# Two orders of loading: which queue carries the first weights and the first tokens, and when layer 1's second slab is fetched

## The reference

```
mix, st = mixing_block(h, pos, w_in, b_in, w_s, b_s, g_mix, w_out, ...)   # starts with x @ w_in + b_in
h = layer_norm(ALPHA * h + mix, ln1_g, ln1_b)
h = layer_norm(ALPHA * h + hier_moe(h, ...), ln2_g, ln2_b)                # top-2 of 16 experts per token
```

## Time and profile before

| What | Value |
|---|---|
| Time, median of 3 runs | 1622.8 us (1620.92 to 1624.57) |
| The profiled execution's own time | 1614.26 us |
| Its span on the core | 1612.4 us |
| Time outside the span in that execution | 1.9 us |
| Mean granted TensorE clock | 0.928 of full speed |
| PE busy | 1427.5 us, 89% of the span |
| DMA, mean over the span | 195 GB/s |

### The profile page before, as it was taken

One profiled execution on the slowest core, in us unless ns is written; L12 is line 12 of the kernel. 1 busy time (PEld: TensorE's weight loads), 2 busy tenths in 40 slices (PEclk: granted clock), 3 DMA queues, 4 the chain that ended last, 5 costly groups with the idle time before them and its releaser, 6 DMA issues.

```text
span 1612.4 us, 20129 instructions
## 1 busy us (share of the span) xinstructions
PE 1427.5 (89%) x7676; PEld 801.9 (50%) x7676; DVE 730.6 (45%) x1525; ACT 313.9 (19%) x651; POOL 129.0 (8%) x118
## 2 busy tenths in 40 slices
PE   7999988889889969999499999888889996999990
PEld 3565555555554535554246454655656454455540
DVE  1294645665583331111437764467458535111116
ACT  1100022323320101121211010333324001221112
POOL 0000200100000040000200011010100001300002
PEclk9999999899889979999799999989988996999995
DMA  9116954457443249999702213553673305799984
GB/s 295 57 50 219 306 149 165 144 161 134 119 163 102 109 158 379 410 407 389 260 31 105 91 48 119 170 203 111 143 159 131 107 0 214 279 403 400 404 331 176
DMA packets 138352, 314.48 MB, mean 195 GB/s; under 512 B 52004, under 2 KB 83748, under 8 KB 117156
## 3 DMA queue, kind: packets, MB, share of 16 engines
q1 hardware_dynamic: 109488, 192.88, 33.8%
q0 software_dynamic: 12672, 86.51, 17.4%
q10 hardware_dynamic: 16116, 34.04, 5.8%
HBM read 266.05 MB, written 47.35 MB: 194 GB/s over the span
## 4 chain that ended last, share of the span: by engine, by line
PE 59%; DVE 18%; issue 14%; DMA 5%; ACT 2%; POOL 1%; ACTq 0%; POOLq 0%; DVEq 0%; SPq 0%
PE ps L1998 9%; PE ps L2344 7%; PE ps L2036 7%; DVE ring L1189 4%; PE ps L2410 4%; DVE z L1189 4%; PE ps L2142 3%; DMA kbuf<-in_cache_k,idx_k 2%; PE ps L2417 2%; PE ps L2447 2%; PE ps L1886 2%; PE ps L2105 2%; PE ps L2071 1%; PE ps L2275 1%; PE ps L1897 1%
## 5 line engine op out<-in xcount | busy, mean ns | idle before, releaser
L1189 DVE TENSOR_TENSOR z<-z,ps 128x512 f32<-128x512 f32 (+1 forms) x102 | 57.6, 585 | 280.8 <-ACT z L890 206.0
L890 ACT ACTIVATE ring<-ps 128x512 f32<-128x512 f32 (+2 forms) x186 | 95.8, 539 | 325.1 <-PE ps L2142 177.5
L2036 PE MATMUL ps<-ring,xT 128*128 128x512 f32 (+1 forms) x384 | 144.4, 535 | 0.8 <-ACT xT L890 0.8
L890 ACT ACTIVATE z<-ps 128x512 f32<-128x512 f32 (+3 forms) x137 | 71.4, 535 | 369.9 <-PE ps L2410 129.1
L2410 PE MATMUL ps<-ring,z 128*128 128x512 f32 x304 | 138.5, 609 | 2.2 <-ACT z L890 1.8
L1998 PE MATMUL ps<-ring,x 128*128 128x512 f32 x320 | 139.1, 593 | 0.0
L2036 PEld LDWEIGHTS ps<-ring,xT 128*128 128x128 f32 x384 | 73.3, 193 | 65.1 <-issue 60.5
L2142 PE MATMUL ps<-tab,kbuf 128*128 128x128 f32 x512 | 86.8, 296 | 13.0 <-DMA kbuf<-in_cache_k,idx_k 8.2
L1998 PEld LDWEIGHTS ps<-ring,x 128*128 128x128 f32 x320 | 60.5, 190 | 74.8 <-issue 74.1
L2410 PEld LDWEIGHTS ps<-ring,z 128*128 128x128 f32 x304 | 57.5, 194 | 69.2 <-issue 68.2
L1189 DVE TENSOR_TENSOR z<-ps,vbuf 128x512 f32<-128x512 f32 (+3 forms) x68 | 36.9, 542 | 112.3 <-PE ps L2036 71.3
(11 more groups left out here) (277 smaller groups left out, 2004.6 us busy)
## 6 DMA issues: line engine op xcount, KB each, us to landing
ring<-in_w SPq DMA_DIRECT2D x114, 1024.0 KB, 9.6
ring<-in_w_in SPq DMA_DIRECT2D x9, 2048.0 KB, 10.3
expert_rows<-zero SPq DMA_DIRECT2D x1, 13056.0 KB, 60.1
expert_rows<-z ACTq DMA_DIRECT2D x19, 512.0 KB, 7.9
z<-expert_rows ACTq DMA_DIRECT2D x17, 512.0 KB, 10.8
ring<-in_w_in SPq DMA_DIRECT2D x6, 1024.0 KB, 8.2
z<-expert_rows ACTq DMA_DIRECT2D x19, 256.0 KB, 8.9
expert_rows<-z ACTq DMA_DIRECT2D x38, 128.0 KB, 6.0
```

The costliest lines, as they stand in the source:

```text
L890: return nc.scalar.activation(out, in_, fn, **kw)
L1189: return V.tensor_tensor(out, a, b, op)
L2036: m = mm(ps[0:n, i % 4, 0:w], xTv[:, k, t * P:t * P + n], slab[at][:, k, 0:w], start=(k == 0), stop=(k == KD - 1))
```

## The change

Two edits of the order of transfers; nothing that is computed changes. At the start of layer 0, the identity columns and token tile 0 are issued by SP ahead of slab 1, and the two halves of slab 0 are issued by ACT ahead of tiles 1 to 3 and the sample tile. At the end of layer 0, SP waits for both gathers of tile 0 (`y_back[0]`) before it fetches layer 1's slab 1.

```
             if layer == 0:
-                w_in_0 = d["w_in"][0].rearrange("(k p) c -> p k c", p=P)
-                kp = KD // PARTS
-                for j in range(PARTS):
-                    sp.dma_start(slab[0][:, j * kp:(j + 1) * kp, :], w_in_0[:, j * kp:(j + 1) * kp, 0:SLAB]).then_inc(s_part[j], 16)
+                sp.dma_start(tab[:, 0:FIRST_TABLES], d["tables"][:, 0:FIRST_TABLES]).then_inc(s_tab, 16)
+                sp.dma_start(x[:, 0, :], d["x_prompt"].rearrange("o (t p) n -> p (o t) n", p=P)[:, 0, :]).then_inc(s_tab, 16)
                 load_slab(0, 1)
                 load_bias(0)
                 load_slab(0, 2)
...
                 sp.wait_ge(h_ps, last_pair * 4 + 3)
+                sp.wait_ge(y_back[0], upto(y_back[0], 16 * TOP_K))
                 load_slab(layer + 1, 1)
                 sp.wait_ge(y_ps, last_pair * 2 + 2)
                 sp.wait_ge(n_done, upto(n_done, 2))
...
             if layer == 0:
-                act.dma_start(tab[:, 0:FIRST_TABLES], d["tables"][:, 0:FIRST_TABLES]).then_inc(s_tab, 16)
+                w_in_0 = d["w_in"][0].rearrange("(k p) c -> p k c", p=P)
+                kp = KD // PARTS
+                for j in range(PARTS):
+                    act.dma_start(slab[0][:, j * kp:(j + 1) * kp, :], w_in_0[:, j * kp:(j + 1) * kp, 0:SLAB]).then_inc(s_part[j], 16)
                 x_p = d["x_prompt"].rearrange("o (t p) n -> p (o t) n", p=P)
-                for t in range(NP):
-                    act.dma_start(x[:, t, :], x_p[:, t, :]).then_inc((s_tab, s_x1, s_x0, s_x0)[t], 16)
+                for t in range(1, NP):
+                    act.dma_start(x[:, t, :], x_p[:, t, :]).then_inc((s_x1, s_x0, s_x0)[t - 1], 16)
                 act.dma_start(x[0:NS, NP, :], d["x_sample"].rearrange("b s n -> (b s) n")).then_inc(s_x0, 16)
                 act.wait_ge(s_tab, 32)
```

## The result

The changed kernel takes 1617.18 us (median of 19 runs, 1605.94 to 1625.71) against 1622.8 us for the kernel before (19 runs beside them, 1608.79 to 1637.39). The ratio is 0.9964, with a 95% interval of 0.9946 to 0.9982: 0.36% faster, where 1619.2 us had been forecast.

The account below looks back on a forecast made before the run. PE holds over half the chain and DMA a twentieth; the edits touch DMA waits at the start and layer boundary. Boundary -3.5 and start -0.1 us took 1622.8 to 1619.2 us, range 1615.0 to 1624.0 (forecast's own 1618.2 to 1620.2).

Parts of the forecast that it names:

- The store: Layer boundary: without slab 1 beside it, layer 0's last store lands in about 2.3 us instead of 5.8.
- The lower bound: Boundary saving at least 2.5 us, since the 512 KB store ahead may trail slab 0 by up to 1 us.
- The sum at the boundary: Layer boundary: the quicker last store starts layer 1 earlier, saving 3.5 us, gathers not helped.
- rival (a): Unit (0, 0) at the boundary: clock rise takes half the gain, 1621.0 (0.10), or adds to it, 1617.5 (0.15).
- Slab 1 lands in time: Layer 1: slab 1, issued about 778, lands at 792.8, needed at 798.0 for unit (1, 0); 5 us to spare.
- its slowest landing in the trace is 14.5 us: Slab 1 in layer 1: the landing time assumed after its later issue, giving 792.8.
- the check from the bytes: Slab 1's landing from 6.0 MB at most at 0.42 MB per us: 14.3 us, so 792.6.
- Tile 1 stays covered: Layer 1: tile 1's gathers return by 786.5, while DVE is busy with tile 0 until 788.3; no cost.
- The start edit: Start of layer 0: same 3.1 MB ahead of tile 1's gate, gain 0.1 us, bounds 0.36 gain to 3.2 loss.
- Rival (b): Start: tile 1 waits behind all of slab 1, costing 3.2 us, total 1622.5; chance 0.06.
- (c): Start: ACT held by its queued issues, first copy of `xT` late, +7.0 us, total 1626.3; chance 0.07.
- Rival (d): Boundary edit does nothing because something else holds the last store; -0.1 us, total 1622.7; chance 0.04.

Follow-up runs that it names:

- 20 fillers and 1: Changed kernel plus 20 unread matmuls after layer 0's last expert block and one behind layer 1 tile 0's transposes: 1614.05 us.
- boundary alone: Kernel before with only slab 1's wait for tile 0's gathers added, start unchanged: 1617.68 us, ratio 0.998.
- tokens early: Changed kernel, SP issuing both slab 0 halves and tile 1, ACT the other tiles after copying tile 0: 1613.29 us; with unread matmuls at the boundary too, 1609.45.
- first group: Runs of each edit alone, slab 1 after the stores, and a slab added at layer 1's end; the kernel before took 1623.7 us beside them.
- 18 fillers: Changed kernel plus 18 matmuls that nothing reads after layer 0's last expert block: 1617.31 us, ratio 0.9966.

## Why the prediction was right, point by point

**The store**, forecast 2.3 instead of 5.8: 2.26 in the changed kernel and 2.25 to 2.57 in every kernel that fetches slab 1 later, 5.33 to 5.80 in every one that doesn't, and slower where a slab was added. This is shown, from both sides. The lower bound, that the 512 KB store ahead might trail slab 0, didn't come in. But that store is where most of the 3.5 us were lost, beside slab 1; the prediction had it only as a risk, beside slab 0. It is the one of `out_full`, ahead of the last store on ACT's own queue. Before, it was issued at 765.43 and took 6.7 us, so it landed at 772.1, 3.1 us after the last store was issued; from 770 to 771 ACT's queue moved 67 packets (0.27 MB) and SP's 68 (0.14 MB), one to one. In the changed kernel it took 3.9 us and landed 0.3 after the last store's issue. So about 2.8 of the 3.5 us come with this store, and the rest with the small ones behind it. That the queues' turns, and not the order in which landings are reported, make the difference is argued from these packets; no run separates the two.

**The sum at the boundary**, forecast -3.5: the restart came 3.4 us earlier over five kernels against three. Between the two profiled runs the gap shrank by 4.6, of which 0.87 is the clock's rise within the unit. The edit doesn't decide that: the unit also took 8.83 and 8.86 with the slab early, and 9.64 and 9.54 with it late. So rival (a) comes with either sign, at most 0.9 us between the two ends, and belongs in the range, not beside it.

**Slab 1 lands in time**, forecast at 792.8 in the prediction's time with 5 us to spare: true that PE doesn't wait, wrong in size. The term that failed is "its slowest landing in the trace is 14.5 us", and the check from the bytes that seemed to confirm it: "6.0 MB at most; at 0.42 MB per us". From issue to landing 6.01 MB were indeed moved, but at 0.348 MB per us: 17.3 us. The rate was read at the start, where whole queues of slab and token rows were waiting. Here it was 0.28 to 0.37 for the first 4 us, with little but gathers moving (from 786 to 789, 257 packets of POOL's queue and 22 of SP's), about 0.42 in the middle, and 0.22 to 0.28 for nearly 4 us from 797 on. What went unseen is that 5 us of reserve were 1.5, and that the next gain at this place runs into it; the kernel with 20 fillers and 1 did, by 0.31.

**Tile 1 stays covered**: right, DVE had no idle time between tiles 0 and 1.

**The start edit**, forecast -0.1 out of -0.36 to +3.2: no gain that shows. Tile 1's transfer landed at 14.1, near the 14.3 that was counted in packets. In the microsecond from 8 to 9 of the changed kernel the two queues moved packets one to one, as in the earlier trace rows, now with rows of 2 KB on both:

```profile
q1 hardware_dynamic: 103, 0.21, 54.1%
q10 hardware_dynamic: 98, 0.20, 51.5%
```

PE began tile 1's transposes at 14.27 to 14.81 in the six kernels with the new order (mean 14.51), and at 14.16 to 14.57 in the three with the old one (mean 14.37). So the 0.1 of gain isn't there, and a loss of 0.1 is within the scatter. Rival (b), +3.2 (its 1.3 MB at 0.42 MB per us make 3.1), didn't happen, nor (c): ACT's issues ended at 4.2, and SP's bias issue, which took 8.00 us behind 4 MB, took 2.09. What the prediction didn't count is PE's own speed: at 14.57 (boundary alone) and 14.72 (after) PE came late and waited for no transfer. The rule of the Trainium skill, in DMA: Bandwidth & Descriptors, section Issuing engines are not separate DMA queues, that spreading issues over engines saves sequencer time only, gave 0.0, and the traces agree.

**Rival (d)** is out by the boundary edit alone: the store went from 5.80 to 2.26.

**The median** came 2.0 us under the forecast, in the case "faster by over 0.2%", which had the largest chance. It lies below the forecast's own range, 1618.2 to 1620.2, next to the 1617.5 of rival (a), though of the 1.75 us that this gives the clock the profiled pair shows 0.87, and no more. The stretches account for 3.4 to 4.6 us of the measured 5.6; the interval of the ratio, 2.9 to 8.8 us, holds both, and the rest isn't explained by any row. The 19 runs of the changed kernel have a granted clock of 0.924 on average and the three groups of before 0.920 to 0.922. At 10 to 14 us for 0.01 that is an estimated 2 to 5 us, part of it the shorter gap itself; but the runs of before that stand beside the changed kernel's have no clock on record, so this stays open. How near to the forecast the median fell is in part luck; what the prediction got right is the 3.5 us at the boundary.

## What to carry to other kernels

A store or gather on the critical path pays for a large prefetch in flight beside it, even one that isn't needed until long after, and a small store pays again for a larger one ahead of it on its own queue; here a prefetch that waited for the chain's first gathers too gave a gap of 31.34, one that waited for its stores alone 33.70. Then work out the prefetch's landing from the rate of the stretch in which it will run, not from the best rate of another, for its reserve is what the next improvement will spend. At the start, where PE begins at the lower clock, data that come earlier can be worth much less than the time by which they come earlier: here PE began some 2.7 us earlier in the two kernels with the tokens early, and 0.64 and 1.55 us of that were left at tile 2.

## What the hardware showed unexpectedly

**Single runs go with the clock.** Over single runs, time and mean granted clock go together: correlation -0.82 over the 19 runs of the changed kernel (0.914 to 0.930, about 10 us for 0.01), -0.93 over the 35 runs of the kernel before in the first group (about 14 us for 0.01), -0.86 and -0.88 in the other two. The two profiled runs differ where the change touches nothing. Stretches of before, in the columns of the earlier trace rows:

```profile
125.00:130.00 5.00, 5.00 (x34) 3.67 (x33) 0.70 (x2) 0.00 (x0) 0.00 (x0) 1.00 0.00 0
130.00:135.00 5.00, 5.00 (x13) 2.22 (x12) 1.43 (x3) 0.00 (x0) 0.00 (x0) 1.00 0.00 0
```

The same stretches of after:

```profile
125.00:130.00 5.00, 5.00 (x31) 4.76 (x30) 0.98 (x2) 0.00 (x0) 0.00 (x0) 0.56 0.00 0
130.00:135.00 5.00, 5.00 (x10) 2.26 (x10) 0.09 (x1) 0.00 (x0) 0.00 (x0) 0.76 0.00 0
```

PE is busy throughout in both, and in one of them the clock falls to 1.2 GHz for a while. Why it does so in dense work stays open; no run here varied it.

**Two short idle times, and the clock fell.** After 15.72 us of dense fillers, idle times of 1.68 and 0.83 us came, and the clock went down; with both filled it stayed up. Both outcomes came twice: units of 8.80 and 8.80 us with 18 fillers, of 7.10 and 7.10 with 20 and 1. Whether one of the two idle times alone would do it, no run shows.

**The clock column is blind at the start.** It shows 1.00 there, yet eight transposes take 1.97 us, as they do at the boundary at 0.50 and against 1.04 later. Durations of a known instruction tell the clock better there. In the four kernels whose PE starts at 4.8 to 5.0, the first eight records of unit (0, 0) take 5.11 to 6.68 us, and in the nine where it starts at 7.5 to 7.8, 4.23 to 5.41: on the whole the early starters do more of the work in the slow stretch.

**The issue of a transfer can last.** SP's issue of the bias took 8.00 us behind 4 MB, 2.09 behind 2.6 MB, and in the changed kernel the issue of the remaining tables, behind slab 2, took 10.23 (6.93 before).
